# Hybrid mLSTM and latent-attention encoder step on one core: own sample keys without mask, squares added before the sum over partitions, head 0's bases on free memory, gate copies ahead of turned tiles

## The reference

```
s = (q_lat . c_kv + q_pe . k_pe) * MLA_SCALE
s = where(visible, s, -inf);  p = softmax(s)          # samples: 256 cached + 16 own keys
rmsnorm(x, w) = x * rsqrt(mean(x*x) + EPS) * w        # mean over the feature axis = partitions
s = (q . k) * exp(b_t - b_s + ig_s - m_t)             # mLSTM weights inside a chunk row
```

## Time and profile before

| | |
|---|---|
| median of 3 runs | 1130.03 us (1128.99 to 1131.24) |
| the profiled execution | 1130.18 us, span 1128.4 us |
| TensorE busy (PE) | 1090.4 us, 97% |
| VectorE (DVE) | 451.1 us, 40% |
| ScalarE (ACT) | 255.0 us, 23% |
| GpSimd (POOL) | 151.8 us, 13% |
| moved by DMA | 162.25 MB, mean 144 GB/s |
| mean granted TensorE clock | 0.989 of full |

### The profile page before, as it was taken

One profiled execution on the slowest core, in us unless ns is written; L12 is line 12 of the kernel. 1 busy time (PEld: TensorE's weight loads), 2 busy tenths in 40 slices (PEclk: granted clock), 3 DMA queues, 4 the chain that ended last, 5 costly groups with the idle time before them and its releaser, 6 DMA issues.

```text
span 1128.4 us, 12597 instructions
## 1 busy us (share of the span) xinstructions
PE 1090.4 (97%) x4708; PEld 710.3 (63%) x4708; DVE 451.1 (40%) x1065; ACT 255.0 (23%) x525; POOL 151.8 (13%) x239
## 2 busy tenths in 40 slices
PE   7999999999968999999999999999999999999997
PEld 5777777777756345453534677777766667656667
DVE  7433343424335567465675000004243333243225
ACT  3211111211134223233231000001123323242221
POOL 5200010100010313213231011011010101000100
PEclk9999999999988999999999999999999999999999
DMA  6223323322363697979979422122211101202202
GB/s 249 103 80 126 111 83 112 116 94 79 125 239 119 256 349 281 361 276 363 371 285 338 164 74 73 38 75 103 86 47 41 59 19 59 82 27 98 70 24 94
DMA packets 44638, 162.25 MB, mean 144 GB/s; under 512 B 4845, under 2 KB 9197, under 8 KB 35634
## 3 DMA queue, kind: packets, MB, share of 16 engines
q1 hardware_dynamic: 44594, 161.65, 39.6%
HBM read 104.42 MB, written 57.21 MB: 143 GB/s over the span
## 4 chain that ended last, share of the span: by engine, by line
PE 89%; DVE 5%; DMA 2%; ACT 1%; issue 1%; POOL 1%; SPq 0%; DVEq 0%; POOLq 0%; ACTq 0%
PE work_b L635 26%; PE work_a L635 23%; PE work_b L1081 5%; PE work_a L897 5%; PE work_a L791 4%; PE bank L683 3%; PE bank L864 2%; PE work_b L847 2%; DVE arena L1893 2%; PE work_a L1151 2%; PE bank L1126 2%; PE bank L1255 1%; PE work_a L1111 1%; PE work_a L873 1%; PE bank L1129 1%; PE work_a L1223 1%
## 5 line engine op out<-in xcount | busy, mean ns | idle before, releaser
L635 PE MATMUL work_b<-arena,ring 128*128 128x320 f32 x832 | 230.7, 433 | 3.7 <-ACT arena L1529 3.7
L635 PEld LDWEIGHTS work_b<-arena,ring 128*128 128x128 f32 x832 | 155.5, 190 | 65.3 <-issue 4.3
L635 PE MATMUL work_a<-arena,ring 128*128 128x320 f32 x640 | 177.7, 436 | 6.5 <-DMA ring<-in_stream 6.5
L635 PEld LDWEIGHTS work_a<-arena,ring 128*128 128x128 f32 x640 | 121.6, 192 | 55.4 <-DMA ring<-in_stream 6.5
L1893 DVE SCALAR_TENSOR_TENSOR arena<-arena,bank 128x512 f32<-128x512 f32 x128 | 87.1, 742 | 66.3 <-PE bank L864 66.3
L1714 DVE COPY arena<-bank 128x384 f32<-128x384 f32 x64 | 28.4, 486 | 130.1 <-PE bank L683 130.0
L635 PE MATMUL work_a<-xc,ring 128*128 128x320 f32 x256 | 70.4, 434 | 1.9 <-ACT arena L1426 1.3
L635 PE MATMUL work_b<-xc,ring 128*128 128x320 f32 x256 | 69.6, 432 | 0.0
L897 PE MATMUL work_a<-arena 128*128 128x512 f32 x128 | 64.4, 615 | 2.8 <-ACT arena L1408 2.8
L635 PEld LDWEIGHTS work_a<-xc,ring 128*128 128x128 f32 x256 | 48.3, 190 | 23.6 <-ACT arena L1426 2.2
L635 PEld LDWEIGHTS work_b<-xc,ring 128*128 128x128 f32 x256 | 48.6, 190 | 20.3
(11 more groups left out here) (289 smaller groups left out, 1355.2 us busy)
## 6 DMA issues: line engine op xcount, KB each, us to landing
ring<-in_stream SPq DMA_DIRECT2D x66, 512.0 KB, 3.5
arena<-in_c SPq DMA_DIRECT2D x32, 1024.0 KB, 8.1
out_s_c<-arena SPq DMA_DIRECT2D x32, 1024.0 KB, 5.7
v_scratch<-arena SPq DMA_DIRECT2D x16, 320.0 KB, 4.7
k_scratch<-arena SPq DMA_DIRECT2D x16, 320.0 KB, 4.5
z_scratch<-arena SPq DMA_DIRECT2D x16, 320.0 KB, 4.8
arena<-k_scratch SPq DMA_DIRECT2D x4, 1280.0 KB, 12.4
arena<-z_scratch SPq DMA_DIRECT2D x4, 1280.0 KB, 9.8
```

The source lines that it names most:

```text
L635: done = mm(halves(buf)[:, a, :], lhs, rhs[:, a * HALF:(a + 1) * HALF], start=first, stop=last)
```

## The change

- **Own keys.** The own part of a sample's scores has the 16 columns of its stream (OWN = 272 columns in all) and no masking product. The mask rows, their load and the copies on GpSimd are gone. VectorE clears two buffers `own_pad` of 240 columns once and scales the 16 own probabilities into their middle, so that a window of 128 columns puts them at the stream's place before they are turned; the other 256 columns are scaled in place.
- **Squares.** GpSimd adds the 2 and the 3 squared tiles (`sum_pairs`), and TensorE sums one tile each.
- **Head 0.** bdk and bdq lie on memory that no store of stage A reads. GpSimd, ScalarE and VectorE begin head 0 ahead of `scratch_written`, and wait for it later. `bd_ready` rises twice a head, after bdk and after bdq. TensorE does two score tiles ahead of the broadcast. The column masks are made after `weight_args(0)`.
- **Weights** of all heads go tile by tile: diagonal and remainder of a tile, then the next; `dmax_ready` and `exp_ready` rise for each tile.
- **Gate copies.** `keep_gate(0)` stands ahead of `turned(1)` on ScalarE.

```diff
+OWN = PAST + STEP
         zh = take(KH, T)
+        bdq, bdk = take(KH, P), take(KH, P)
...
-        bdq = take(KH, P)
-        bdk = take(KH, P)
...
-        ones16 = take16(P)
-        own_keys = take16(STREAMS, P)
-        mask_rows = take(STREAMS * P)
...
-        pexp_f = [take(3 * P) for _ in range(2)]
+        pexp_f = [take(OWN) for _ in range(2)]
+        own_pad = [take(2 * P - STEP) for _ in range(2)]
...
             def project_head(h):
-                pe.wait_ge(bd_ready, h + 1)
+                pe.wait_ge(bd_ready, 2 * h + 2 if h else 1)
...
                     project_keys(h)
+                    pe.wait_ge(bd_ready, 2)
                     project_queries(h)
...
                 if h == 0:
                     pe.wait_ge(bc_out, 1)
+                    pe.wait_ge(G.bfree[0], c.all(G.bfree[0], ahead=1))
+                    pe.wait_ge(cols_ready, 4)
...
             project_head(0)
-            for t in range(3):
+            for t in range(2):
                 scores(0, t)
...
-            for t in range(3, TT):
+            for t in range(2, TT):
                 scores(0, t)
-            pe.wait_ge(G.bfree[0], c.all(G.bfree[0], ahead=1))
-            pe.wait_ge(cols_ready, 4)
...
             def mean_square(sq_tiles, n):
-                for k in range(n):
-                    pe.wait_ge(squares, c.next(squares))
-                    for a in range(2):
-                        last = mm(bank[a][:, 0:HALF], ones_f[:], sq_tiles[:, k, a * HALF:(a + 1) * HALF],
-                                  start=k == 0, stop=k == n - 1)
+                pe.wait_ge(squares_summed, c.next(squares_summed))
+                c.skip(squares, n)
+                for a in range(2):
+                    last = mm(bank[a][:, 0:HALF], ones_f[:], sq_tiles[:, 0, a * HALF:(a + 1) * HALF],
+                              start=True, stop=True)
...
+                mine = slice(SEQ + b * STEP, SEQ + (b + 1) * STEP)
                 for r in range(RT):
-                    mm(bank[s][:, PAST:PAST + P], qb[s][:, r, :], ckv[:, r, SEQ:T], start=r == 0, stop=False)
-                mm(bank[s][:, PAST:PAST + P], qb[s][:, 2, :], kpe[:, SEQ:T], start=False, stop=False)
-
-                mm(bank[s][:, PAST:PAST + P], ones16[0:1, :], own_keys[0:1, b, :],
-                                    start=False, stop=True).then_inc(E.bfill[s], c.up(E.bfill[s]))
+                    mm(bank[s][:, PAST:OWN], qb[s][:, r, :], ckv[:, r, mine], start=r == 0, stop=False)
+                mm(bank[s][:, PAST:OWN], qb[s][:, 2, :], kpe[:, mine],
+                   start=False, stop=True).then_inc(E.bfill[s], c.up(E.bfill[s]))
...
-            scratch_written(act)
             keep_q(0)
...
+            scratch_written(act)
             keep_m(0)
...
             def weights(h):
-                act.wait_ge(dmax_ready, h + 1)
                 for t in range(TT):
+                    act.wait_ge(dmax_ready, TT * h + t + 1)
                     a_s = cols[:, 0, t, h:h + 1]
                     own = pt[:, OFF[t]:OFF[t] + P]
-                    nc.scalar.activation(own, own, ACT.Exp, bias=a_s, scale=-1.0).then_inc(act_own, c.up(act_own))
-                for t in range(NP - 1):
...
+                    raised = exp_ready if t >= NP - 1 else act_own
+                    nc.scalar.activation(own, own, ACT.Exp, bias=a_s, scale=-1.0).then_inc(raised, c.up(raised))
+                    if t < NP - 1:
+                        op = nc.scalar.activation(pt[:, OFF[t] + P:OFF[t] + WID[t]], mbw[:, (t + 1) * P:SEQ],
+                                                  ACT.Exp, bias=a_s, scale=-1.0)
+                        op.then_inc(exp_ready, c.up(exp_ready))
...
                 for t in range(NP):
+                    if t == 2:
+                        keep_gate(0)
                     if t:
                         turned(t - 1)
-                    if t == 2:
-                        keep_gate(0)
...
-            scratch_written(dve)
             keep_k(0)
...
             def weighted_scores(h, t):
                 dve.wait_ge(score_mm, TT * h + t + 1)
-                if t == 0:
-                    dve.wait_ge(exp_ready, h + 1)
+                dve.wait_ge(exp_ready, TT * h + t + 1)
...
+            dve.wait_ge(bc_out, 1)
+            weight_args(0)
+            column_masks()
+            for t in range(NP):
+                weighted_scores(0, t)
             stream_weights(0)
-            weight_args(0)
-            for t in range(TT):
-                weighted_scores(0, t)
+            weighted_scores(0, NP)
             stream_queries(0)
...
+            def own_probabilities(s):
+                dve.wait_ge(E.bfree[s], c.next(E.bfree[s]))
+                v.reciprocal(rinv[:, s:s + 1], rsum[:, s:s + 1]).then_inc(dve_own, c.up(dve_own))
+                dve.wait_ge(dve_own, c.all(dve_own))
+                for n, (dst, part) in enumerate(((own_pad[s][:, P - STEP:P], slice(PAST, OWN)), (pexp_f[s][:, 0:PAST], slice(0, PAST)))):
+                    raised = prob_ready if n else dve_own
+                    op = v.tensor_scalar(dst, pexp_f[s][:, part], rinv[:, s:s + 1], None, ALU.mult)
+                    op.then_inc(raised, c.up(raised))
...
+            head_basis(0)
             scratch_written(pool)
-            head_basis(0)
...
+            def sum_pairs(tiles, n):
+
+                pool.wait_ge(squares, c.next(squares))
+                for k in range(1, n):
+                    pool.wait_ge(squares, c.next(squares))
+                    raised = squares_summed if k == n - 1 else pool_own
+                    g.tensor_tensor(tiles[:, 0, :], tiles[:, 0, :], tiles[:, k, :], ALU.add).then_inc(raised, c.up(raised))
+                    pool.wait_ge(raised, c.all(raised))
+
+            sum_pairs(lsq, RT)
             pool.wait_ge(Dd.free[0], KD // 2 + 2)
             swap_halves()
+            sum_pairs(csq, QT)
```

More of the change, by code:

```diff
@@ L363, in program @@
         lrstd, qrstd = take(T), take(T)
-        ones16 = take16(P)
-        own_keys = take16(STREAMS, P)
-        mask_rows = take(STREAMS * P)
         pexp = [take(SEQ) for _ in range(2)]
+        keys_c = take(10, P)
         k0 = top[0]
@@ L377, in program @@
         mx, nmx, rsum, rinv = take(2), take(2), take(2), take(2)
-        keys_c = take(10, P)
         area[0] = xc[:].rearrange("p a b -> p (a b)")
@@ L570, in _ @@
             sp.wait_ge(y_ready, 2 * HEADS)
-            for dst, name in ((rope_c, "cos"), (rope_s, "sin"), (uv, "uv"), (mask_rows[0:1], "masks")):
+            for dst, name in ((rope_c, "cos"), (rope_s, "sin"), (uv, "uv")):
                 sp.dma_start(dst, i[name]).then_inc(misc_in, c.up(misc_in, 16))
@@ L1039, in sample_scores @@
                 own = keys[b % 3]
-                if b == 0:
-                    pe.wait_ge(masks_ready, c.next(masks_ready))
                 pe.wait_ge(keys_in[b % 3], c.next(keys_in[b % 3], step=16))
@@ L1206, in sample_turn @@
                 pe.wait_ge(E.bfree[2 + s], c.all(E.bfree[2 + s]))
-                for q in range(3):
-                    last = nc.tensor.transpose(bank[2 + s][:, q * P:(q + 1) * P], pexp_f[s][:, q * P:(q + 1) * P], ident[:])
+                at = (STREAMS - 1 - b) * STEP
+                for q, part in enumerate((pexp_f[s][:, 0:P], pexp_f[s][:, P:2 * P], own_pad[s][:, at:at + P])):
+                    last = nc.tensor.transpose(bank[2 + s][:, q * P:(q + 1) * P], part, ident[:])
                 last.then_inc(E.bfill[2 + s], c.up(E.bfill[2 + s]))
@@ L1582, in _ @@
                 stage_e(p)
-            exponentials(E, 0, pexp_f[0], 3 * P)
+            exponentials(E, 0, pexp_f[0], OWN)
             for b in range(STREAMS):
                 if b + 1 < STREAMS:
-                    exponentials(E, (b + 1) % 2, pexp_f[(b + 1) % 2], 3 * P)
+                    exponentials(E, (b + 1) % 2, pexp_f[(b + 1) % 2], OWN)
                 if b + 2 < STREAMS:
@@ L1793, in _ @@
             op.then_inc(dve_own, c.up(dve_own))
+            scratch_written(dve)
             dve.wait_ge(exp_rows, c.next(exp_rows))
@@ L1807, in _, with column_masks @@
             dve.wait_ge(G.bfree[0], c.all(G.bfree[0]))
[L1808 to L1818 removed]
+            def column_masks():
+                op = v.tensor_tensor(wz, bmask[:, STREAMS:].unsqueeze(2).to_broadcast([P, 2, HEADS]),
+                                     cols[:, 2, NP].unsqueeze(1).to_broadcast([P, 2, HEADS]), ALU.mult)
+                op.then_inc(cols_ready, c.up(cols_ready))
+                op = v.tensor_tensor(wq_mask, bmask[:, 0:STREAMS].unsqueeze(1).to_broadcast([P, HEADS, STREAMS]),
+                                     wi_col.unsqueeze(2).to_broadcast([P, HEADS, STREAMS]), ALU.mult)
+                op.then_inc(cols_ready, c.up(cols_ready))
+                op = v.tensor_tensor(wb, bmask[:, 0:STREAMS].unsqueeze(1).to_broadcast([P, HEADS, STREAMS]),
+                                     cols[:, 2, NP].unsqueeze(2).to_broadcast([P, HEADS, STREAMS]), ALU.mult)
```

(20 more changed lines are left out.)

32 lines of the change are left out of this document (6 added, 26 removed).

## The result

| | median of the runs | lowest to highest | profiled execution | its span | mean granted clock |
|---|---|---|---|---|---|
| before | 1129.51 us (4 runs) | 1128.75 to 1131.24 | 1130.18 us | 1128.4 us | 0.989 |
| after | 1104.13 us (4 runs) | 1102.33 to 1105.48 | 1102.33 us | 1100.6 us | 0.998 |

The ratio of the two is 0.9772, with a 95% interval of 0.9752 to 0.9792. By it the changed kernel is 25.7 us faster (25.4 by the two medians), where 24.9 were forecast.

What follows compares the result with a forecast made beforehand. TensorE, busy 97% of the span, was taken to bound the kernel. Head 0 16.0, squares 3.2, gates 3.7 and own keys 2.0 sum to 24.9 us off 1130.0: 1105.1 us, own range 1103 to 1108, wider range 1101.5 to 1113 (0.85).

Steps and rivals of the forecast that it cites:

- rival 1: Head 0: the clock falls once more, with TensorE idle between 328 and 334.5; some 3.4 us, giving 1108.5; chance 0.16.
- First gap: Head 0's start: bases no longer wait for stores, so TensorE starts 7.2 us earlier and first scores come 7.6 us earlier.
- The middle: Head 0, scores to first values: no gap before the key sums, which run at full clock; 7.0 us.
- The rest of head 0: Head 0, first values to first update: full clock instead of half, 2.0 us.
- Squares: Sums of squares: 12 TensorE records go, GpSimd's additions stay hidden; 3.2 us, ends 1.7 and 3.2.
- Gates: Gate tiles: all three TensorE waits for ScalarE's gate copy go; 3.7 us, ends 2.4 and 3.7.
- Own keys: Samples' scores: six 16-column records at 0.11 us replace the own part, 0.25 us a stream; 2.0 us over eight.
- Rival 3: Own sample keys: small records are cheap, 2 to 4.5 us more gain than forecast, about 1102; chance 0.09.
- The clock row at half level in head 0: Sign against the prediction: it is wrong if the clock row shows 0.50 anywhere in head 0.
- Rival 2: Head 0: ScalarE's late copies and VectorE's chain hold it, costing 7 us more, 1112.1; chance 0.12.
- Rival 4: The four heads: transfers set the pace and eat the gain, 1140 at 290 GB/s; chance 0.03.
- Rival 5: Gate or squares do not give, as a new wait replaces theirs; up to 3.7 + 1.5 us, to 1110; chance 0.06.

Runs made afterwards that it cites:

- e3: Only the gate copy moved ahead of the turned tiles, against the kernel before: 1124.63 us, ratio 0.9961.
- e7: 64 columns in place of 16 in the own part of each stream's scores, against the changed kernel: one execution, 1105.56 us.
- e8: The changed kernel run again, the same program, for its spread: 1106.20 us, ratio 0.9792 to the kernel before.
- e12: Three unread products filling TensorE's idle time in head 0, against the changed kernel with own and cached keys joined in 272-column products: 1099.75 us.
- e6: VectorE copies two of head 0's eight key products instead of four, ScalarE six, against the changed kernel: 1105.40 us, ratio 0.9782 to the kernel before.
- e9: VectorE copies six of head 0's eight key products instead of four, ScalarE two, against the changed kernel: 1104.28 us, ratio 0.9779 to the kernel before.
- e5: Only the squares pre-added on GpSimd, against the kernel before: 1126.15 us, ratio 0.9972.
- e2: Only head 0's bases on free memory, moved waits and split bd_ready, without tile-by-tile weights, against the kernel before: 1121.66 us, ratio 0.9937.
- e4: Only the own sample keys with 16 columns and the padded own probabilities, against the kernel before: 1125.98 us, ratio 0.9975.

## Why the prediction was right

The time (1104.13 against 1105.1) came out as the forecast had it, though in part by luck, from two errors that cancel. In an execution in which the clock stays the steps gave 27.15 us and not 24.9 (the other 0.70 of the 27.85 are no part of the change): the terms were right or a little short. And rival 1 takes some of it back in most executions.

- *First gap, forecast 7.2 at the key products and 7.6 at the first scores.* 7.30 and 7.78 from the turned sums on. The step held, with the idle in two pieces as forecast: 1.50 + 0.69 us, where 2.8 were reckoned.
- *The middle, forecast 7.0, to the first values.* 6.98. TensorE reached the sums at 347.29 (forecast 347.8), VectorE's last weighted scores were out at 348.22 (349.5), and the values began at 349.67 (350.2). This holds for the mechanism as a whole; what each of its three edits is worth alone was not run. k of head 0 was the late one, as named: ScalarE waited 1.21 us for it, until 348.70, and nobody waited for ScalarE.
- *The rest of head 0, forecast 2.0.* 2.00. The sum was 16.6 and I took off 0.6 for semaphores in a row: measured 16.76. That allowance had no row behind it, and is a term that was mis-sized.
- *Squares, forecast 3.2.* 3.23, and GpSimd's last sum stood at 792.1, where TensorE asked for it at 797.36: hidden.
- *Gates, forecast 3.7.* 4.36. The term took the waits alone. Each also cost 0.25 us of overlap with the work before and behind it (e3).
- *Own keys, forecast 2.0.* 2.8. The record was taken at 0.11 us from the row of 128 columns and is 0.098, which is 0.07 of the 0.10 us a stream that the term was short; 0.02 stand in the records behind it. Rival 3, small records by their columns, is out: 16 and 64 columns cost 0.59 and 0.61 us in six records (e7). The Trainium skill's page "TensorE: Matmul & The Clock Gate" (Back-to-back issue gap) has 1 to 64 columns at one cost, about 60 cycles, a floor of 25 ns, or 62 ns where the decoding in hardware is off. The trace agrees that the cost is one, not on its size: 98 ns, with new weights ahead of each record. The Trainium skill's same page (LDWEIGHTS) has a load cost its columns over 1.2 GHz, by which 128 take 107 ns (an estimate): nearer, as forecast, and a little high. The two clearings took 0.52 us and were hidden (VectorE 1001.75, TensorE 1005.33).
- *Rival 1, the clock falls once more in head 0.* It was given 0.16 and is by the mean clock the commoner case: seven of the nine executions of this program lie below 0.998. The clock row at half level in head 0, which the prediction named as a sign that it is wrong, is absent from the first trace and stands in that of e8. Its price was right, 3.35 us where 3.4 were reckoned. Its cause was wrong: idle between 328 and 334.5 was to bring it, and it fell later and without idle (e8, e12); only in e6, where TensorE's wait was made longer, did it fall in the wait. For this reason the nine times, 1102.24 to 1108.89 us, lie on both sides of the forecast.
- *Rival 2, the copies.* They do set the first scores (e9), by 1.6 us in the kernel as it is, not by 7. *Rival 4, the transfers:* the stretch of the heads has 328 GB/s at a share of 0.88, as before, and the stage took 377.21 us where it took 377.48. *Rival 5:* no new wait took the place of an old one (e3, e5).

The range, 1101.5 to 1113, held every execution of both sets.

## What to carry to other kernels

A wait on the bounding engine costs more than its idle time: the overlap with the work on either side goes with it (0.25 us beside a wait of 1.22), and, if it is long, the clock. A small product costs its record, so make it ride in a larger one with the same weights: the 16 columns in records of their own cost a stream 0.59 us more than within the product of 256, 0.50 at the scores and 0.09 in the records behind them. When the time of one program is spread by more than its steps explain, print the mean clock of each execution beside its time before judging a gain of a few microseconds: e9's first scores came 1.6 us earlier, and its median could not show it.

## What the runs showed of the hardware

The granted clock fell from 2.4 to 1.2 GHz while TensorE was busy without a pause (8.00 of 8.00 us, mean clock 0.57, in e12), in some executions of a program and not in others. The Trainium skill's page "TensorE: Matmul & The Clock Gate" (HAM oscillation) describes the fall as the effect of a wait of the engine. The falls of before (idle from 326 to 333.7 and from 355.7 to 360.2) and of e6 fit that. Those of e2 and e7 to e12, and the second ones of e3 and e4, do not: they came before TensorE's wait, or with none near. I had expected neither that, nor that filling the idle time would change nothing.
